# Doubled keys and a joined state step in a chunked recurrence, and rounded products for a mask and key sums, in a hybrid encoder trunk

## The reference

```python
# branch A
log_rest = jnp.where(mask, jax.nn.log_sigmoid(-z), 0.0)
after = lax.cumsum(log_rest, axis=3, reverse=True) - log_rest
attn = jnp.where(mask, jnp.exp(jax.nn.log_sigmoid(z) + after), 0.0)
...
# branch B, one step
sa = jnp.einsum('bhvk,bhk->bhv', S, -kk_t)
S = (S * w_t[:, :, None, :] + sa[..., None] * (kk_t * a_t)[:, :, None, :]
     + v_t[..., None] * k_t[:, :, None, :])
return S, jnp.einsum('bhvk,bhk->bhv', S, r_t)
```

## Time and profile before

| what | value |
|---|---|
| median of 3 runs | 2036.55 us (2035.19 to 2040.31) |
| profiled execution | 2034.68 us, its span 2032.9 us, 1.8 us lie around it |
| busy PE, DVE, ACT, POOL | 98%, 74%, 59%, 3% of the span |
| recurrence of layer 0 | 192.73 to 275.50 us |
| the same in layer 1 | from 827.19 us |
| branch A of layer 0 | 122.26 to 161.47 us |

### The profile page before, as it was taken

The page is one execution under the profiler, slowest core; times in us unless marked ns, Lnnn a source line. Parts: engine busy times, 40 slices in busy tenths (PEclk is TensorE's granted clock), DMA queues, the critical chain, the costliest instruction groups (busy, mean ns, idle before and its releaser), DMA issues.

```text
span 2032.9 us, 36044 instructions
## 1 busy us (share of the span) xinstructions
PE 2001.4 (98%) x15296; PEld 1761.3 (87%) x15296; DVE 1496.4 (74%) x1311; ACT 1199.0 (59%) x1076; POOL 53.6 (3%) x36
## 2 busy tenths in 40 slices
PE   8999999999999999999999999999999999999998
PEld 6978999999998888899988888888888888888886
DVE  6656356765455766438578898888889889898896
ACT  5454453543343545445467777777777777777675
POOL 0003100000000001200000000000000000000000
PEclk9999999999999999999999999999999999999999
DMA  7432035444442322105459899898998989899895
GB/s 239 172 111 97 4 133 201 166 166 172 187 162 106 142 106 86 41 27 225 179 224 380 344 358 373 323 372 336 369 367 335 373 334 364 349 359 372 326 376 199
DMA packets 75038, 485.60 MB, mean 239 GB/s; under 512 B 13480, under 2 KB 14632, under 8 KB 17192
## 3 DMA queue, kind: packets, MB, share of 16 engines
q1 hardware_dynamic: 73816, 481.93, 61.3%
q10 hardware_dynamic: 1104, 1.92, 0.3%
HBM read 482.08 MB, written 1.74 MB: 238 GB/s over the span
## 4 chain that ended last, share of the span: by engine, by line
PE 92%; DVE 4%; ACT 2%; DMA 1%; issue 1%; POOL 0%; ACTq 0%; SPq 0%; DVEq 0%
PE PS L576 26%; PE PS L578 25%; PE PS L577 25%; PE PS L956 6%; DVE area L1910 1%; PE PS L1282 1%; PE PS L1291 1%; DVE WL L1910 1%; ACT WH L1442 1%; PE PS L914 1%; DMA ring<-in_weights 1%; PE PS L731 1%; DVE YEL L2515 0%; PE PS L1358 0%; PE PS L847 0%
## 5 line engine op out<-in xcount | busy, mean ns | idle before, releaser
L1910 DVE TENSOR_TENSOR WL<-ring,WH 128x2048 fp32r<-128x2048 f32 x410 | 934.4, 2290 | 218.0 <-ACT WH L1442 109.3
L1442 ACT ACTIVATE WH<-ring 128x2048 fp32r<-128x2048 f32 x336 | 643.1, 1916 | 158.5 <-PE PS L578 149.0
L576 PE MATMUL PS<-WH,XGH 128*128 128x512 f32 x896 | 353.7, 395 | 0.2 <-DVE XGL L1910 0.2
L578 PE MATMUL PS<-WL,XGH 128*128 128x512 f32 x896 | 349.7, 390 | 0.0
L577 PE MATMUL PS<-WH,XGL 128*128 128x512 f32 x896 | 349.1, 390 | 0.0
L578 PE MATMUL PS<-XL,WH 128*128 128x272 f32 (+1 forms) x704 | 202.5, 288 | 0.0
L1434 ACT ACTIVATE WH<-ring 128x2048 fp32r<-128x2048 f32 x74 | 141.3, 1910 | 102.0 <-PE PS L578 102.0
L578 PEld LDWEIGHTS PS<-WL,XGH 128*128 128x128 f32 x896 | 168.1, 188 | 35.8
L576 PEld LDWEIGHTS PS<-WH,XGH 128*128 128x128 f32 x896 | 168.3, 188 | 34.6 <-DVE WL L1910 0.5
L577 PEld LDWEIGHTS PS<-WH,XGL 128*128 128x128 f32 x896 | 168.4, 188 | 33.5
L576 PE MATMUL PS<-WH,HTH 128*128 128x512 f32 x448 | 176.7, 394 | 0.6
(11 more groups left out here) (350 smaller groups left out, 3432.7 us busy)
## 6 DMA issues: line engine op xcount, KB each, us to landing
ring<-in_experts SPq DMA_DIRECT2D x336, 1024.0 KB, 6.6
ring<-in_weights SPq DMA_DIRECT2D x114, 1024.0 KB, 6.9
ring<-in_weights SPq DMA_DIRECT2D x4, 576.0 KB, 4.4
ring<-in_weights SPq DMA_DIRECT2D x4, 512.0 KB, 4.0
cst<-in_consts SPq DMA_DIRECT2D x1, 1731.0 KB, 7.4
hT<-in_stream ACTq DMA_DIRECT2D x2, 544.0 KB, 7.0
out<-area SPq DMA_DIRECT2D x4, 256.0 KB, 2.0
bias_line<-lin SPq DMA_DIRECT2D x1, 672.0 KB
```

What stands on the lines that cost most here:

```text
L576: pe.matmul(o, lh, rh, start=first, stop=False, skip_group_check=True)
L578: return pe.matmul(o, lh, rl, start=False, stop=last, skip_group_check=True)
L1442: act.activation(WH[(BASE + j + 1) % 3][:, :], ring[b][:, 2048 * (j % 2):2048 * (j % 2) + 2048], ACT.Copy).then_inc(S("w_hi"), 1)
L1910: tt = lambda o, a_, b_, op: dve.tensor_tensor(o, a_, b_, op)
```

## The change

- Constants: `sbmask` is gone, 128 spare columns come in; VectorE copies `negsuffix`, `negones`, `hidden` and `ident` once into rounded form (`exact`).
- Branch A: `hidden` is added to the scores by PE, as a rounded product with the identity ahead of `zscores`; the multiplication by `sbmask` and the pass `hidden_keys` are gone; exp reads PSUM. `softplus` writes a rounded copy SPH and its remainder SPL, and `key_sums` runs over both as rounded products.
- Branch B: POOL copies AI and K side by side (`double_keys`, four copies of 64 partitions x 256 for each chunk), so that one set of 64x128 weights (`products_m`) gives what two sets gave, each head in its own bank; `turn_rows` uses the same weights, and the values are turned into the other half of the partitions. `state_step` is one set over 128 rows. `right_side` and `outputs_known` are each split in two steps. `open_rows` reads PSUM, `open_turned` is three operations. POOL applies the causal mask in four operations, and the order of pass c is new.

```diff
+                    for g in range(2):
+                        pe.matmul(PS[:, b + g, 0:432], exact("ident"), exact("hidden"), start=True, stop=False, skip_group_check=True)
...
+                    for part in (SPH, SPL):
+                        for g in range(2):
+                            pe.matmul(PS[:, b + g, 0:432], exact("negsuffix"), part[:, g, :], start=False, stop=False, skip_group_check=True)
+                    for part in (SPH, SPL):
+                        for g in range(2):
+                            pe.matmul(PS[:, b + g, P:T], exact("negones"), part[:, g, T:416], start=False, stop=False, skip_group_check=True)
+                            for o in (2 * P, 400):
+                                ins = pe.matmul(PS[:, b + g, o:o + 16], exact("negones"), part[:, g, 416:432], start=False, stop=part is SPL,
+                                                skip_group_check=True)
...
+                    pe.wait_ge(S("keys_doubled"), nth(l, c))
+                    for p in range(4):
+                        for g in range(2):
+                            ins = pe.matmul(PS[:, g, 2 * CH * p:2 * CH * p + 2 * CH], doubled_keys(c)[heads[g], p, :, :].rearrange("p x b -> p (x b)"), RK[heads[g], :, p, cc],
+                                            start=True, stop=True, skip_group_check=True)
...
+                    both(1, 0, lambda g, p: BHT[s_][:, g, p, :], lambda g, p: UV[s_][:, g, p, :]).then_inc(S("r_s"), 1)
...
-                products_h(0)
-                products_b(0)
-                gate_steps(3)
+                products_n(0)
+                gate_steps(1)
+                products_m(0)
+                gate_steps(2)
                 turn_rows(0)
                 gate_steps(3)
                 level_product(0, 1)
-                pe.wait_ge(S("r_tc"), nth(l, 0))
-                products_b(1)
+                products_n(1)
+                pe.wait_ge(S("r_tc"), 2 * nth(l, 0))
+                products_m(1)
...
                     if c > 1:
-                        products_b(c)
                         level_product(c - 1, 4)
-                        products_h(c)
+                        products_m(c)
                         level_update(c - 1, 4)
                         level_product(c - 1, 5)
-                        level_product(c, 1)
                         turn_rows(c)
                         level_update(c - 1, 5)
-                        right_side(c - 1)
+                        level_product(c, 1)
+                        right_values(c - 1)
+                    outputs_values(c - 1)
+                    if c > 1:
+                        right_state(c - 1)
                     level_update(c, 1)
                     solve(c - 1)
+                    if c > 1:
+                        outputs_state(c - 1)
                     level_product(c, 2)
                     state_step(c - 1)
+                    outputs_solved(c - 1)
                     level_update(c, 2)
-                    outputs_known(c - 1)
                     level_product(c, 3)
-                    outputs_solved(c - 1)
+                    if c + 1 < NCH:
+                        products_n(c + 1)
                     level_update(c, 3)
...
+                    for g, sem in enumerate(("r_bc", "r_hc")):
+                        act.activation(BH[c % 2][:, g, :, :, :].rearrange("p a x b -> p (a x b)"), PS[:, g, :], ACT.Copy).then_inc(S(sem), 1)
...
+                    link(pool, pool.tensor_copy(o[0:HD, :, 0, :], AI[0:HD, :, cc]), "pool_chain")
+                    link(pool, pool.tensor_copy(o[0:HD, :, 1, :], K[0:HD, :, cc]), "pool_chain")
+                    link(pool, pool.tensor_copy(o[HD:P, :, 0, :], K[HD:P, :, cc]), "pool_chain")
+                    pool.tensor_copy(o[HD:P, :, 1, :], AI[HD:P, :, cc]).then_inc(S("keys_doubled"), 1)
...
                 for n in range(LATE, len(FILLS)):
+                    if n == LATE + 4:
+                        pool.wait_ge(S("g_done"), 4 * l + 4)
+                        pool.wait_ge(S("c_z"), at("c_z", l, N_UNITS[l] - 1))
+                        double_keys(0)
+                        double_keys(1)
                     pool.wait_ge(S("t_hi"), len(FILLS) * l + n + 1)
...
+                    link(pool, pool.tensor_tensor(upper, upper, bc(causal[HD:P, 1, :], [HD, 4, CH], 1), ALU.mult), "pool_chain")
+                    pool.tensor_tensor(lower, lower, bc(causal[0:HD, 1, :], [HD, 4, CH], 1), ALU.mult).then_inc(S("r_hm"), 1)
+                    pool.wait_ge(S("r_hm"), nth(l, c))
+                    for g in range(2):
+                        m = BH[s_][:, g, :, 0, :]
+                        ins = pool.tensor_tensor(m, m, bc(causal[:, 0, :], [P, 4, CH], 1), ALU.mult)
+                    ins.then_inc(S("r_bm"), 1)
...
+                    for g, o in enumerate((slice(0, HD), slice(HD, P))):
+                        dve.wait_ge(S(("r_bc", "r_hc")[g]), nth(l, c))
+                        ins = tt(TT[s_][o, :, :], BH[s_][o, g, :, 1, :], bc(C("turned")[o, :], [HD, 4, CH], 1), ALU.mult)
+                    v(ins)
                     tt(TT[s_][:, :, :], TT[s_][:, :, :], one, ALU.add).then_inc(S("r_open_t"), 1)
...
                 power(0, 3)
                 for c in range(1, NCH):
                     if c > 1:
-                        open_rows(c)
                         power(c - 1, 4)
+                        power(c - 1, 5)
                         open_turned(c)
-                        power(c - 1, 5)
-                    power(c, 1)
+                        power(c, 1)
...
+                    v(dve.tensor_copy(SPH[:, :, :], spA[:, :, :]))
+                    tt(SPL[:, :, :], spA[:, :, :], SPH[:, :, :].bitcast(F32), ALU.subtract).then_inc(S("sp_done"), 1)
```

More of the change, by code:

```diff
@@ L950, in _, with both @@
                 heads = slice(0, HD), slice(HD, P)
-                def both(bank, col, lhs, rhs, n=CH, first=None, start=True):
+                def both(bank, col, lhs, rhs, first=None, swapped=False):
                     for p in range(4):
-                        for r in heads:
-                            ins = pe.matmul(PS[r, bank, n * p + col:n * p + col + n], lhs[r, p], rhs(r, p),
-                                            start=start if first is None else first and p == 0, stop=True, skip_group_check=True)
-                    return ins
+                        for g in range(2):
+                            ins = pe.matmul(PS[heads[1 - g if swapped else g], bank, CH * p + col:CH * p + col + CH], lhs(g, p), rhs(g, p),
+                                            start=True if first is None else first and p == 0, stop=True, skip_group_check=True)
+                    return ins
@@ L960, in columns, with of_head, products_n, products_m @@
+                def of_head(x_):
+                    return lambda g, p: x_[heads[g], p, :]
                 def columns(c):
                     return slice(c * CH, (c + 1) * CH)
-                def products_b(c):
-                    s_, cc = c % 2, columns(c)
+                def products_n(c):
+                    cc = columns(c)
+                    both(2 + c % 2, 0, of_head(KK[:, :, cc]), of_head(AI[:, :, cc])).then_inc(S("r_n"), 1)
+                def products_m(c):
+                    cc = columns(c)
@@ L1020, in turn_rows @@
                 def turn_rows(c):
[L1021 to L1024, removed]
+                    pe.wait_ge(S("r_hc"), nth(l, c))
+                    for p in range(4):
+                        for g in range(2):
+                            pe.matmul(PS[:, g, CH * p:CH * p + CH], doubled_keys(c)[heads[g], p, :, :].rearrange("p x b -> p (x b)"), C("stack")[heads[g], :],
+                                      start=True, stop=True, skip_group_check=True)
+                    for p in range(4):
+                        for g in range(2):
+                            ins = pe.matmul(PS[heads[1 - g], g, 256 + CH * p:256 + CH * p + CH], V[heads[g], p, columns(c)], C("stack")[heads[g], :],
+                                            start=True, stop=True, skip_group_check=True)
+                    ins.then_inc(S("r_t"), 1)
                 def level_product(c, w):
@@ L2041, in _ @@
                 attention_pads()
+                if l == 0:
+                    dve.wait_ge(S("setup"), 16 * N_SETUP)
+                    for name, src in (("negsuffix", "negsuffix"), ("negones", "negones"), ("hidden", "hidden"), ("ident", "ident")):
+                        dve.tensor_copy(exact(name), C(src))
                 piece_low(5, 6, 7)
```

203 lines of the change are left out of this document (109 added, 94 removed).

## The result

The changed kernel takes 2038.89 us (median of 12 runs, 2036.45 to 2046.88), the kernel before 2036.12 beside it; the ratio is 1.0019 (95% interval 1.001 to 1.0028). Forecast were 2039 and "within 0.3%". The total came out right, but two of its terms did not, and their errors had opposite signs. (The difference of the medians is 2.8 us.) The profiled execution took 2036.45, its span 2034.7, with the granted clock at 0.996 as before.

A forecast was written before the change was run, and what follows sets the result against it. PE, carrying 92% of the chain, was taken to bound the kernel. Terms +6.8 + 0.4 - 0.5 - 4.0 = +2.7 us took the profiled 2034.68 to 2037.4; the runs' median lies 1.9 above, so 2039, range 2029 to 2047.

The forecast's parts named there:

- The passes: Branch B's recurrence, six passes: work 0.9 less, waits +2.06, a period of 15.8 us for 14.64, +6.8 in all.
- both waits: PE's waits in a pass: 0.74 us for ACT's copies before level product 5, 1.39 for DVE's open_turned, held by POOL's masks.
- Rival 1: Branch B: POOL does not hold DVE back, passes of 14.6 us, 2032.4 in all; chance 0.17.
- rival 2: Faster: switches of array shape cost nothing and POOL holds nobody, passes of 14.2 us, 2027 in all; chance 0.13.
- Rival 3: Slower: POOL paces branch B, at the masks and fill 12, +14.6 us, 2051 in all; chance 0.12.
- Rival 4: Slower: PE waits at each array-shape switch for the last product's full end, 4.7 us more, 2044 in all; chance 0.06.
- Pass 1 and tail: Branch B's first loop pass and end: a state_step set less, second copies ahead of solutions more, +0.2 us a layer, +0.4.
- The openings: Stretches before the recurrence's loop, with POOL's eight copies before fill 12: layer 0 +0.4, layer 1 -0.9, together -0.5 us.
- The three savings: Opening behind level product (0, 1): one set fewer twice and 0.88 for 1.76 once, taken as -1.0 us.
- Branch A: Eight pairs: cheaper key_sums against the mask as a PE product, -4.0 us; bounds -6.2 and -0.7.
- the last pair's wait: Branch A: PE's wait at the pair with no scores ahead to cover DVE's longer chain, 0.3 us a layer.
- Rival 5: Branch A: rounded products of few columns are slow, so branch A gives nothing, +6.7 us, 2043 in all; chance 0.04.

The follow-up runs named there:

- masks_late: The changed kernel with POOL's four masks of a chunk held until open_turned is done and, from chunk 2, DVE's mask of level 2: 2035.86 us, ratio 0.9999.
- act_order: The changed kernel with ACT copying the inverse of level update 4 between the two banks of products_m instead of behind both: 2036.94 us, ratio 1.0005.
- before_late: The kernel before with POOL's two masks of a chunk put off behind open_turned and, from chunk 2, DVE's mask of level 2: 2039.62 us, ratio 1.0017.
- fill_dve: The kernel before with late POOL masks, rounded key sums (mask on DVE) and layer 1's low part of fill 11 made by DVE: 2033.59 us, ratio 0.9993.
- a_alone: The kernel before with only the changes to branch A and the constants: 2031.69 us, ratio 0.9995.
- b_alone: The changed kernel with the changes to branch A and the constants taken back: 2043.47 us, ratio 1.0029.
- split_double2: The changed kernel with POOL doubling chunk 0's keys before fill 12 and chunk 1's only between fills 12 and 13: 2038.37 us, ratio 1.0026.

## Why the prediction was right

*The passes.* Right in mechanism, in both waits and in the switches. The change takes 0.9 of work out of a pass, by the forecast's own count, and puts 1.7 to 2.0 into it, 1.5 of it the two waits. Measured +1.04, +0.80 and +0.78 a pass, +5.2 for six, forecast +6.8. Both waits were mis-sized: ACT's (0.55 for 0.74), since PE came to it later (0.05 behind 238.41, 2.7 us behind the pass's start, for 2.47), while ACT was ready nearly when forecast (3.2); and DVE's (0.98 for 1.39). DVE started `open_turned` when it should (4.31 us behind the pass's start, forecast 4.38), but its operations ended 0.87 apart, where I had 1.05 and 1.08: at 4.87, 5.75 and 6.61, for 4.8, 5.85 and 6.93. masks_late shows DVE's part, act_order ACT's.

*Rival 1* (POOL does not hold DVE) is refuted by the masks that end 0.28 before DVE's operations and by masks_late. With it falls *rival 2*, which also had POOL hold nobody. *Rival 3* (POOL paces all) fell with copies of 0.4. *Rival 4:* a switch from 64x64 into 64x128 weights gives a distance of 0.15 between starts, for 0.05 between sets of one shape, and out of them 0.20: 0.25 more for the pair, where I had 0.18, far from the full length of the last product that this rival asks for. (The Trainium skill, TensorEngine Tiling (Array Packing), section Key Properties, says that changing the tiling mode drains TensorE; the trace agrees that a switch costs, about 0.1 to 0.15 each.)

*Pass 1 and tail:* -0.29 a layer (2.33 less 2.62) for +0.2. *The openings:* -0.3 for -0.5, out of two errors in layer 0: up to level product (0, 1) it took 0.4 more than before, not 1.3, as the copies were 0.4 and not 0.6; behind it 0.3 less, not 1.0. (The three savings that the forecast names there add up to 1.8; it took 1.0 without saying why.)

*Branch A* is the step that failed: "-4.0" was -0.8. It has three parts: a rounded product of 16 columns, for which I said "at most that, at least half" of 0.10 and took 0.075, was 0.106, and 144 columns cost 0.10, not 0.07 (0.37 a pair, 3.0 in all); the mask took 0.60, not 0.49 (0.9 in all); and the 0.6 allowed for the last pair's wait never came, which goes the other way. My lower bound, -0.7, held it. Rival 5 ("Rounded products of few columns are slow") was true in the main. That the total was right is luck: this miss (+3.2) and those of the recurrence (-2.4) went opposite ways, and stretches that the change does not touch came out 1.7 us shorter in the trace. At equal clock the change costs 4.0 +- 0.4, where the sum said 2.7.

## What to carry to other kernels

Where a step saves PE's instructions in a chain of dependent small products, count the waits between its pieces first: here 48 instructions less a pass made it 0.8 to 1.0 us longer. POOL work that nobody needs for a pass belongs where no DVE operation with two SBUF inputs stands on the critical chain; a wait on POOL's side took back 2.6 us at equal clock. Look there in the kernel before, too: the same masks cost it 1.4 us by the stretches, which the reading of a single pass did not show. And before a float32 product is split in two rounded ones, look at its columns: at 432 the split nearly halved the cost (0.79 for 1.45 us), at 16 nothing was won. Where differences are some 0.2%, look at the clock of the runs as well as at their times: here before_late had less work than the kernel before, a lower mean clock, and the longer median.

## What the runs showed of the hardware

- POOL and DVE hold one another in both directions: DVE's operation ends 0.28 us after POOL's, POOL's copy 0.26 us after DVE's (1.52 for 0.39). It holds for DVE operations with both inputs in SBUF; one with an input in PSUM took its usual 0.42 beside a POOL mask. The Trainium skill (SBUF — State Buffer, section 🔬 SBUF: two separate sides) says that of a DVE operation with two SBUF inputs and a GpSimd operation that reads SBUF, whichever starts first has the shared pair of ports for its whole instruction; these traces agree.
- The clock. In every trace PE stands for 1.7 to 2.8 us in layer 1 for a fill (2.8 in all but fill_dve's, between starts); where it stood 2.8, the granted clock is near 0.5 behind it, the lower of its two levels (1.2 of 2.4 GHz). In the kernel before, then in the changed one:

```profile
820.50:823.00 2.50, 2.44 (x11) 2.44 (x12) 1.43 (x2) 0.00 (x0) 0.01 (x1) 0.51 0.00 0
```
```profile
820.50:823.00 2.50, 2.50 (x13) 2.40 (x13) 0.56 (x2) 0.00 (x0) 2.19 (x6) 0.50 0.03 7
823.00:826.00 3.00, 3.00 (x17) 2.79 (x15) 0.00 (x0) 1.64 (x4) 1.12 (x3) 0.52 0.00 0
```

  Rounded products start 0.213 apart there, for 0.12 behind it. How long it lasts differs from trace to trace: from 822 to 828 us the mean clock was 0.84 before and 0.68 after, and that accounts for the 1.25 us of the first table. From 700 to 725 us it was 0.93 before and 1.00 after, 1.5 of the -1.78.
- A wait of PE is not needed for it. From 1000 to 1040 us PE is busy for 39.3 to 40.0 us in every trace; the mean clock there is 1.00 in those of the kernel before, the changed kernel, a_alone and act_order, and 0.79 to 0.96 in the ten others.
- Over a kernel's runs the mean clock lay between 0.9927 (b_alone) and 0.9961 (the kernel before beside fill_dve), 5.1 us by the line above. It was lower than that of the kernel before beside it in b_alone and in all eight kernels from split_double2 to fill_dve, and not in a_alone, masks_late and act_order. What sets it was not found.
